# A one-core diffusion backbone step: instructions moved in two norms, the input projection, the start of the scans and the head normalization

## What is computed

```python
def rmsnorm(x, w):
    return x * lax.rsqrt(jnp.mean(x * x, axis=-1, keepdims=True) + NORM_EPS) * w

h = rmsnorm(x, norm_w[1]) * (1.0 + m[:, :, 4]) + m[:, :, 3]     # before the mixer, and alike before the FFNs
u = h @ w_in                                                     # 1024 -> 4480 columns, the input map
r, k, v = split(short_conv(u[..., :OFF_WD], conv_rkv))
kk = kk / jnp.maximum(jnp.sqrt(jnp.sum(kk * kk, -1)), 1e-12)     # per head of 64
def step(S, inp):                                                # two directions, 8 heads, 64 x 64 state
    sa = einsum('bhij,bhj->bhi', S, kk_t)
    S = S * w_t - sa * (kk_t * a_t) + v_t * k_t
    o = einsum('bhij,bhj->bhi', S, r_t)
o = (o - mu) * lax.rsqrt(var + GN_EPS) * lnx_w + lnx_b           # per head
o = (o + bonus) * g
y_four = fourier_mix(f, grid) @ w_fourier
```

## Time and profile before

| | us |
|---|---|
| median of 3 runs | 2956.28 (2952.41 to 2957.88) |
| the profiled execution, its own time | 2961.8 |
| its span | 2960.0 |
| TensorE (PE) busy, matmuls | 2812.5 (95% of the span) |
| VectorE (DVE) busy | 1542.9 (52%) |
| ScalarE (ACT) busy | 804.4 (27%) |
| GpSimd (POOL) busy | 468.5 (16%) |
| first FFN | about 62 to 928 |
| norm and input map | 928 to 1432 |
| scans | 1432 to 1748 |
| head normalization | 1748 to 1829 |
| Fourier, merge, second norm | 1829 to 2124 |
| second FFN, final norm | 2124 to 2960 |

### The profile page before, as it was taken

The page is one execution under the profiler, slowest core; times in us unless marked ns, Lnnn a source line. Parts: engine busy times, 40 slices in busy tenths (PEclk is TensorE's granted clock), DMA queues, the critical chain, the costliest instruction groups (busy, mean ns, idle before and its releaser), DMA issues. The chain is left out here.

```text
span 2960.0 us, 53461 instructions
## 1 busy us (share of the span) xinstructions
PE 2812.5 (95%) x21936; PEld 2680.2 (91%) x21936; DVE 1542.9 (52%) x2777; ACT 804.4 (27%) x1409; POOL 468.5 (16%) x561
## 2 busy tenths in 40 slices
PE   7999999999998999999799977999899999999998
PEld 3999999999997989999688865899799999999997
DVE  4456656655536345632477858455633333333335
ACT  4211111111115233444256544222511111111111
POOL 4100011011005001222233414122400000000001
PEclk9999999999999999999799999999999999999999
DMA  6122222222202434444654432321111111111112
GB/s 271 57 72 72 85 85 83 73 84 79 71 15 95 131 116 143 147 144 147 197 121 106 92 134 87 118 91 45 44 43 43 43 42 38 38 39 38 40 42 71
DMA packets 187199, 257.67 MB, mean 87 GB/s; under 512 B 99073, under 2 KB 136961, under 8 KB 185377
## 3 DMA queue, kind: packets, MB, share of 16 engines
q1 hardware_dynamic: 173280, 227.86, 23.7%
q0 software_dynamic: 12608, 27.48, 2.8%
q10 hardware_dynamic: 1152, 0.07, 0.0%
HBM read 200.23 MB, written 55.12 MB: 86 GB/s over the span
## 5 line engine op out<-in xcount | busy, mean ns | idle before, releaser
L868 DVE SCALAR_TENSOR_TENSOR x<-bank,gate,x 128x128 f32<-128x128 f32 (+1 forms) x832 | 409.9, 515 | 199.8 <-PE bank L998 199.2
L1053 ACT ACTIVATE act_out_ffn<-bank 128x384 f32<-128x384 f32 x132 | 64.9, 491 | 1268.8 <-PE bank L969 1268.8
L1056 DVE TENSOR_TENSOR g_ffn<-act_out_ffn,bank 128x384 f32<-128x384 f32 x132 | 73.2, 554 | 617.1 <-ACT act_out_ffn L1053 617.1
L969 PE MATMUL bank<-h_hi_ffn,wlo_a_ffn 128*128 128x384 f32 x1056 | 358.6, 340 | 14.1 <-DVE h_lo_ffn L663 7.3
L969 PE MATMUL bank<-h_lo_ffn,whi_a_ffn 128*128 128x384 f32 x1056 | 356.4, 337 | 0.0
L969 PE MATMUL bank<-h_hi_ffn,whi_a_ffn 128*128 128x384 f32 x1056 | 356.3, 337 | 0.0
L969 PE MATMUL bank<-h_hi_ffn,whi_b_ffn 128*128 128x384 f32 x1056 | 354.9, 336 | 0.0
L969 PE MATMUL bank<-h_hi_ffn,wlo_b_ffn 128*128 128x384 f32 x1056 | 354.9, 336 | 0.0
L969 PE MATMUL bank<-h_lo_ffn,whi_b_ffn 128*128 128x384 f32 x1056 | 354.9, 336 | 0.0
L998 PE MATMUL bank<-g_hi_ffn,wlo_d_ffn 128*128 128x384 f32 x1056 | 354.0, 335 | 0.0
L998 PE MATMUL bank<-g_lo_ffn,whi_d_ffn 128*128 128x384 f32 x1056 | 352.8, 334 | 0.0
(11 more groups left out here) (301 smaller groups left out, 4929.2 us busy)
## 6 DMA issues: line engine op xcount, KB each, us to landing
ada_beside_ffn<-in_ada_w POOLq DMA_DIRECT2D x96, 256.0 KB, 3.5
raw_a_ffn<-in_ffn_w SPq DMA_DIRECT2D x44, 512.0 KB, 4.4
raw_b_ffn<-in_ffn_w SPq DMA_DIRECT2D x44, 512.0 KB, 5.1
raw_d_ffn<-in_ffn_w SPq DMA_DIRECT2D x44, 512.0 KB, 3.7
raw_in<-in_w_in SPq DMA_DIRECT2D x35, 512.0 KB, 5.1
mix<-row_out SPq DMA_DIRECT2D x23, 576.0 KB, 3.2
sc_ar<-streams SPq DMA_DIRECT2D x36, 256.0 KB, 3.8
gates<-mix SPq DMA_DIRECT2D x16, 576.0 KB, 5.1
```

The source lines that it names most:

```text
L868: ins = nc.vector.scalar_tensor_tensor(xs, kit.banks[4 + d % 4][:, a:b], kit.gate[:, gate, d, cond:cond + 1], xs, ALU.mult, ALU.add)
L969: mm = nc.tensor.matmul(kit.banks[2 * slot + j][:, 0:CH], w[q][:, par, cols], v[:, k, toks], start=(k == 0 and m == 0), stop=(k == ku - 1 ...
L1053: return self.nc.scalar.activation(out, a, ACT.Silu)
L1056: self.nc.vector.tensor_tensor(g32, act_out, b, ALU.mult).then_inc(g32_ready, 1)
```

## The change

Nothing that is computed changes. Instructions are moved on their engines or between them, in five places:

- Norms ahead of the input map and of the second FFN: the low parts of chunks 1 and 2 are all VectorE's; the reciprocal of chunk 1 goes ahead of low(7), that of chunk 2 behind low(15).
- Input map: the four operand stores go ahead of the row store in SP's loop; the fold goes ahead of the low part of the next weights; of the divisions (thirds 0 and 1 in window 3, third 2 in window 4) third 1 moves to window 4.
- Start of the scans: units 1 and 2 are loaded behind unit 0 in `first_loads`, units 3 and 4 behind `n_in[0]`; the masks of units 0 to 2 and then two whole lane chains go first on VectorE; the read of the first inverses is shared by SP and ScalarE; the wait for the states moves on GpSimd.
- Heads: r of the first tile comes by thirds, v ahead of the gate's operands, the Fourier input after tile 1; a Sqrt activation is run beforehand; affine goes ahead of the Fourier channels on ScalarE, which come one step later (on TensorE too); `rk_ones` is made one by one behind `weighted`.
- The heads' product with the inverse (L2320) stays on VectorE.

```diff
@@ -237,7 +237,7 @@
-        engine = self.nc.vector if m % 2 else self.nc.gpsimd
+        engine = self.nc.vector if m % 2 or m >= KT else self.nc.gpsimd
@@ -270,16 +270,21 @@
     def vector(self, dve):
+        self.reciprocal(dve, 1)
         self.low(dve, 7)
+
+        dve.wait_ge(self.h_ready[0], KT // 2)
         for m in range(KT, NC * KT):
-            if m % KT == 0:
-                if m > KT:
-
-                    dve.wait_ge(self.xn_ready, KT)
-                self.reciprocal(dve, m // KT)
+            if m == 2 * KT:
+
+                self.low(dve, m - 2)
+                self.low(dve, m - 1)
+                dve.wait_ge(self.xn_ready, KT)
+                self.reciprocal(dve, 2)
             self.scaled(dve, m)
-            if (m - 2) % 2 and m - 2 > KT - 1:
+            if KT <= m - 2 < 2 * KT - 2 or m - 2 >= 2 * KT:
                 self.low(dve, m - 2)
+        self.low(dve, NC * KT - 2)
         self.low(dve, NC * KT - 1)
@@ -345,7 +350,7 @@
             if m % 2:
                 self.odd_full(pool, m)
-            else:
+            elif m < KT:
                 self.low(pool, m)
@@ -1168,6 +1173,11 @@
                     sp.dma_start(raw[:, par], kit.dram["w_in"][ORDER[p + 2]]).then_inc(loaded[par], 16)
+                ct, w = window(p)
+                if w == 4:
+                    store_operands(ct, 1)
+                if w == (4 if ct == CT - 1 else 5):
+                    store_operands(ct, 0)
                 if conv_index(p) is not None:
@@ -1216,11 +1226,6 @@
-                ct, w = window(p)
-                if w == 4:
-                    store_operands(ct, 1)
-                if w == (4 if ct == CT - 1 else 5):
-                    store_operands(ct, 0)
@@ -1455,10 +1460,10 @@
             for p in range(J_END):
+                if p and J_F <= ORDER[p - 1] < J_GATE:
+                    fold(p - 1)
                 if 2 <= p + 1 < J_END:
                     low(dve, p + 1)
-                if p and J_F <= ORDER[p - 1] < J_GATE:
-                    fold(p - 1)
@@ -1474,9 +1479,9 @@
                 if w == 3 and ct + 1 < CT:
-                    divide(ct + 1, (0, 1))
+                    divide(ct + 1, (0,))
                 if w == 4 and ct + 1 < CT:
-                    divide(ct + 1, (2,))
+                    divide(ct + 1, (1, 2))
@@ -1693,13 +1704,17 @@
             sp.dma_start(masks[:], kit.dram["masks"]).then_inc(S["masks_in"], 16)
+            load_unit(sp, 1)
+            load_unit(sp, 2)
             for d in range(2):
...
         def sync(sp):
-            for k in range(1, 5):
-                load_unit(sp, k)
+
+            sp.wait_ge(n_in[0], 16)
+            load_unit(sp, 3)
+            load_unit(sp, 4)
@@ -1712,13 +1727,9 @@
-                    for c in range(2):
+                    for c in range(2 if k else 1):
                         for b in range(4):
...
+                            sp.dma_start(*inverses_of(k, c, b)).then_inc(x_in[k % 2], 16)
@@ -1840,6 +1850,10 @@
                     level(m + 2, 0)
+                if m + 2 == 0:
+                    act.wait_ge(x_out[0], 16)
+                    for b in range(4):
+                        act.dma_start(*inverses_of(0, 1, b)).then_inc(x_in[0], 16)
@@ -1935,7 +1949,19 @@
-            for m in slots:
+            def lanes(l):
+                for s in range(6, -1, -1):
+                    row(l, s)
+                for step in range(4):
+                    corner(l, step)
+
+
+            for k in range(3):
+                for r, e in ((0, 0), (0, 1), (1, 0), (1, 1)):
+                    masked(k, r, e)
+            lanes(0)
+            lanes(1)
+            for m in slots[3:]:
@@ -2209,12 +2237,17 @@
             for ct in range(CT):
-                sp.dma_start(r[:, ct], mix[ct]).then_inc(r_loaded[ct], 16)
+                if ct == 0:
+
+                    for c in range(NC):
+                        sp.dma_start(r[:, 0, part(c)], mix[0][:, part(c)]).then_inc(r_first[c], 16)
+                else:
+                    sp.dma_start(r[:, ct], mix[ct]).then_inc(r_loaded[ct], 16)
+                sp.dma_start(v[:, ct], mix[2 * CT + ct]).then_inc(v_loaded[ct], 16)
...
-                sp.dma_start(v[:, ct], mix[2 * CT + ct]).then_inc(v_loaded[ct], 16)
-                if ct == 0:
+                if ct == 1:
                     sp.dma_start(cs[:], kit.dram["dft_features"]).then_inc(s["f_in"], 16)
@@ -2269,7 +2302,7 @@
-            skewed([(0, sums), (1, bonus), (1, variance), (2, gate), (2, channels)])
+            skewed([(0, sums), (1, bonus), (1, variance), (2, gate), (3, channels)])
@@ -2305,7 +2338,9 @@
-            skewed([(0, square), (1, root), (2, channels), (2, affine), (3, high)])
+
+            nc.scalar.activation(one_root[:], kit.eps[:, 0:1], ACT.Sqrt)
+            skewed([(0, square), (1, root), (2, affine), (3, channels), (3, high)])
@@ -2331,13 +2366,12 @@
         def gpsimd(pool):
-            for ct in range(CT):
-                nc.gpsimd.tensor_scalar(rk_ones[:, ct], cst.pair_ones, kit.col("r_k", ct), None, ALU.mult)\
-                    .then_inc(s["rk_ones"], 1)
-
             def weighted(m):
...
                 nc.gpsimd.tensor_tensor(at(kd_sum, m), at(r, m), at(kd_sum, m), ALU.mult).then_inc(s["rk_ready"], 1)
+                if m % NC == 0:
+                    nc.gpsimd.tensor_scalar(rk_ones[:, ct_of(m)], cst.pair_ones, kit.col("r_k", ct_of(m)), None, ALU.mult)\
+                        .then_inc(s["rk_ones"], 1)
```

More of the change, by code:

```diff
@@ L1605, in scans @@
     names = ("masks_in", "preset", "states_in", "states_out", "am_done", "am_ready", "n_out", "n45_ready",
-             "n_out_act", "lane_step", "turned_block", "full6", "free6", "full7", "free7", "u_done", "u_act", "u_dve", "z_done",
+             "n_out_act0", "n_out_act1", "lane_step", "turned_block", "full6", "free6", "full7", "free7", "u_done", "u_act", "u_dve", "z_done",
              "z_ready", "zg_ready", "o_done", "o_ready", "a_done", "a_out", "wa_done", "wa_out", "wy_done")
@@ L1668, in blocks_of, with inverses_of @@
                     nkr[at:at + BL, k % NKR, :, :, c, 0, BL * b:BL * b + BL].rearrange("s e x t -> s (e x) t"))
+        def inverses_of(k, c, b):
+            at = 64 * c + BL * b
+            return (xy16[at:at + BL, k % 2, :, :, BL * b:BL * b + BL].rearrange("s w h t -> s (w h) t"),
+                    x_blocks[k].rearrange("w (h c b) (s t) -> c b s (w h) t", c=2, b=4, t=BL)[c, b])
         def load_ar(sp, k):
@@ L1714, in sync @@
                         sp.wait_ge(S["full7"], f7(k - 2, "y32"))
-                    for c in range(2):
+                    for c in range(2 if k else 1):
                         for b in range(4):
-                            at = 64 * c + BL * b
-                            sp.dma_start(xy16[at:at + BL, k % 2, :, :, BL * b:BL * b + BL]
-                                         .rearrange("s w h t -> s (w h) t"),
-                                         x_blocks[k].rearrange("w (h c b) (s t) -> c b s (w h) t", c=2, b=4, t=BL)[c, b]
-                                         ).then_inc(x_in[k % 2], 16)
+                            sp.dma_start(*inverses_of(k, c, b)).then_inc(x_in[k % 2], 16)
                 if m in (1, 2):
@@ L1740, in gpsimd @@
                 nc.gpsimd.memset(lane_x[:, p, 0, 0:BL * (BL + 1):BL + 1], 1.0).then_inc(S["preset"], 1)
-            pool.wait_ge(S["masks_in"], 16)
-            pool.wait_ge(S["states_in"], 32)
             def grown(m, c):
+                if m == 0 and c == 0:
+                    pool.wait_ge(S["states_in"], 32)
                 if m or c:
@@ L1759, in lanes_in @@
                 if k < 2:
-                    pool.wait_ge(S["n_out_act"], 64 * (k + 1))
+                    pool.wait_ge(S[f"n_out_act{k}"], 64)
                 if k >= 2:
@@ L1764, in lanes_in @@
                     .then_inc(n_in[k % 2], 16)
-            grown(0, 0)
             for m in slots:
@@ L1770, in gpsimd @@
                     blocks_out(m + 4)
-                if 0 < m + 1 < NU:
+                if live(m + 1):
                     grown(m + 1, 0)
@@ L1829, in scalar @@
                     for b in range(4):
-                        act.dma_start(*blocks_of(m + 4, 1, b)).then_inc(S["n_out_act"], 16)
+                        act.dma_start(*blocks_of(m + 4, 1, b)).then_inc(S[f"n_out_act{m + 4}"], 16)
                 if live(m - 1) and first_visit(m - 1):
@@ L2190, in head_norm @@
     r_loaded, v_loaded = ([kit.sem(f"hn_{q}_loaded{ct}") for ct in range(CT)] for q in "rv")
+    r_first = [kit.sem(f"hn_r_first{c}") for c in range(NC)]
     with ExitStack() as ctx:
@@ L2196, in head_norm @@
         f, cs = buf("fo_f", [P, FG, T]), buf("fo_cs", [P, 2 * FD])
+        one_root = buf("hn_one_root", [P, 1])
         steps = CT * NC
@@ L2233, in bonus @@
             def bonus(m):
-                pe.wait_ge(s["rk_ones"], CT)
+                pe.wait_ge(s["rk_ones"], ct_of(m) + 1)
                 pe.wait_ge(s["rk_ready"], m + 1)
@@ L2333, in gpsimd @@
```

(8 more changed lines are left out.)

## The result

The changed kernel takes 2939.9 us in the median of 8 runs (2933.6 to 2948.0), the kernel before 2957.1 of 8 (2951.5 to 2959.6): ratio 0.9949, interval 0.9936 to 0.9962, some 15 us faster (11 to 19). The forecast was 35.5 and the range ended at 2938: the sign was right, the size twice too large. The profiled execution took 2933.6, the fastest of its eight, against 2961.8 before, which is above all eight of its own kernel. So the two traces lie 28.2 us apart where the medians lie 17.2; a part of what they show as gain is two executions at opposite ends.

What follows compares the result with a forecast made beforehand. TensorE, busy 95% of the span, was taken as the bound, so only its waits and the slow clock behind them pay. 6 + 4.5 + 10.5 + 5 + 9.5 = 35.5 us, from median 2956.3 to 2920.8; range 2910 to 2938.

Steps and rivals of the forecast that it cites:

- Heads, -9.5 forecast: Head normalization: -3.4 from a shorter steady loop and -6 from its first steps; bounds -4 and -11.
- The loop, -3.4 forecast: Heads' steady loop: affine first shortens it by 0.5 until VectorE's sum of 4.9 to 5.0 bounds it; -3.4.
- the -6 at the start: Heads' first steps: roots 1.9 earlier, and the Fourier input's wait of 4.2 no longer stops the steps behind it; -6.
- Input map, -10.5 forecast: Projection: two single TensorE waits, 2.7 and 3.1, go with the half-clock stretches behind them; -10.5, bounds -5.8 and -12.
- (a): Projection, position 14: one division moves behind the low part; the wait of 2.7 and its half-clock stretch go, -4.1.
- (b): Projection, position 16: operand stores ahead of the row store, fold ahead of the low; wait of 3.1 and stretch go, -6.3.
- Rival 3: Projection: row stores queue behind four operand stores each and ScalarE cannot write the row buffer; 2962 or more, chance 0.03.
- rival 4: TensorE's clock: the waits go, but half-clock stretches come elsewhere; 8 less gain, 2929, chance 0.08.
- Start of the scans, -5 forecast: Scans' start: earlier loads and masks, shared read of the inverses, slot 0 about 5 earlier; bounds +2 and -9.
- rival 2: Scans' start gives 0, twelve masks delaying the first lane chain; Fourier input late, heads -5.5; 2930, chance 0.15.
- Norms, -10.5 forecast: Norms ahead of the projection, -6, and of the second FFN, -4.5: low parts and reciprocals come earlier on VectorE.
- The rule against the change: Norms: GpSimd's SBUF interfaces are shared with VectorE, contending with two-input instructions; by it the norms go by the slow end.

Runs made afterwards that it cites:

- `lane_early`: The changed kernel with the first lane chain ahead of the masks of unit 2 on VectorE; median 2936.0 us, ratio 0.9937 to the kernel before.

## Why the prediction was wrong

- **Heads, -9.5 forecast, -1.0 found: the largest miss, in all three of its parts.**
  - The loop, -3.4 forecast, 0 found. "VectorE's own sum of 4.9 to 5.0 bounds it" took the product at a fixed price, though the row for it stood at 0.91 and elsewhere at 0.56. I asked whether GpSimd slows VectorE in the norms and did not ask it in the heads, where all three GpSimd instructions have two inputs. The product went to 1.38 and the step stayed at 5.5.
  - The Fourier input, part of the -6 at the start. The input was issued 4.5 to 5.9 us behind the heads' first matmul instead of 2.3, some 3 later, as forecast. But "that wait no longer stops the steps behind it" was wrong: TensorE still waited 1.9 to 4.6 for it (4.2 before), where the prediction asked for under 1. By the last reciprocal the heads gained 3.2 to 5.0 in all.
  - The end, which the sum put at nothing. The channels' later place costs 3.6 there.
- **Input map, -10.5 forecast, -6.9 found (3 by medians, interval wide).** (a) and (b) were right: both waits went. Rival 3's mechanism, which I priced at nothing below a landing of 16 us, came once, behind the stores of direction 1, with the sign that the prediction had named, a wait of ScalarE for `mix<-row_out`. The false step was "its buffer is wanted again two tiles, 24.6 us, after the last use". It is wanted at the start of the position after next, one tile after its last eviction ends (1144.7 to 1157.2), and the move used up just that: the store was issued 0.4 before ScalarE asked for its end (1162.92 less 5.71 is 1157.21), and an ordinary landing of 6 us was enough. Behind its 1.8 the clock fell in seven of eleven traces, rival 4's mechanism; at the prediction's own prices for the stretches that is 1.5 in the mean, an estimate, and with the 1.8 it makes most of the 3.6 that are missing.
- **Start of the scans, -5 forecast, -2.5 found.** Counted from the scans' first matmul, the chain of unit 1 ended at 31.3 to 33.2 instead of 36.3, 3.1 to 5.0 earlier, as forecast. But the stage does not end with it: it ends with the inverses of unit 0, whose chain ended at 24.7 to 26.6 against 25.1. It began right behind the twelfth mask, at 18.0 to 19.9 against 18.0, as rival 2 says. What came is the shared read, some 1.5 of 1.9, and 1.6 for masks already done. The prediction's other fear, SP still busy with units 3 and 4 when the inverses are ready, did not come in the change, but in `lane_early`.
- **Norms, -10.5 forecast, -9.6 found.** Sizes right; the reason half wrong. I had 3.6 for the order and 0.9 and the pace for the engine; the order alone is worth nothing. The half-clock stretch, whose going was priced at 1.6, got shorter and moved.
- **The rule against the change** was asked in the wrong stage, as the heads show. In the norms VectorE's lows beside GpSimd's TENSOR_SCALAR took 0.55, as assumed, though `scaled` went to 0.86 in two of eight tiles, and GpSimd's full parts took 0.90 to 1.69 where the sum had 1.
- The chance of 0.94 for faster was sound. The likeliest total was the sum of five terms, four of which stood three quarters of the way or more to their high ends. The range ended at 2938 although the low ends added up to 2945, and 2939.9 lies between. The sign "slot 0 begins 25 to 30 us earlier" does not follow from the sum either: the terms up to there make 21.5, and it began 15.1 earlier in the trace after.

What stays open: whether the order of the reciprocals adds anything once the lows are VectorE's, and why the slots differ by 6.9 between executions.

## What to carry to other kernels

When an edit lets one engine start earlier, list what its instructions will now lie beside. Here a VectorE product with two SBUF inputs took 0.56 by itself and up to 1.38 where it started just behind a GpSimd TENSOR_TENSOR, and a loop bound by VectorE gave back what the shorter dependency had gained. When something is moved back in a queue, count how late it already was, and not only how long it takes. When a chain is shortened, ask which chain the next stage waits for, and whether the queue behind it is free. A sum of terms, each argued to be nearly whole, should be cut before it is a forecast. Two traces of two executions do not give a difference below the spread of either kernel.

## What the runs showed of the hardware

A wait of TensorE of 1.8 or 1.9 us at the same place in the map was followed by a stretch at 0.50 of 3.4 or 6.8 us in seven of eleven traces (6.8 us in the window above) and by none in four. Waits of 3.1 ahead of chunk 2 of the norm were followed by one of 3.4 in all five traces that had them.

A TENSOR_TENSOR on VectorE with two SBUF inputs of 128x384 took 0.56 us by itself. Where it started while a GpSimd TENSOR_TENSOR was under way, it ended 0.41 to 0.42 us after that one, and so took up to 1.39. GpSimd's own took 1.00 where it had started first, and 1.31 or 1.32 where 0.45 to 0.47 us of VectorE's product were still to run when it started.
